# Shared SBUF stretches filled ahead across three phases, smaller weight pieces for three chunks, and the sample tokens taken first

## What is computed

```python
xn = rmsnorm(x, p['g_mix'][l])
proj = xn @ p['w_in'][l]
mq, mk, mv, mo, mi, mf, aq, ak, av, gt = split_proj(proj)
li = mi + b_igate;  lf = log_sigmoid(mf + b_fgate)
h_m, C, n, m = mlstm(mq, mk, mv, li, lf, st_C, st_n, st_m, m_chunk)
h_m = rms(h_m) * g_mhead * sigmoid(mo)
q, k = rope(aq, pos), rope(ak, pos)
h_a, nk, nv = swa_attend(q, k, av, st_k, st_v, buf_valid, a_sinks, a_block)
ga, gb = split(sigmoid(gt))
x = x + (ga * (h_m @ w_a) + gb * (h_a @ w_b)) @ w_out
y, cbuf = conv_ffn(rmsnorm(x, g_ffn), st_conv, w_up, w_conv, b_conv, w_down)
x = rmsnorm(x + y, g_final)
```

## Time and profile before

| | us |
|---|---|
| median of 3 runs | 3063.32 (3062.82 to 3065.42) |
| the profiled execution | 3068.29 |
| its span, first to last instruction | 3066.3 |
| PE busy | 2922.9 (95%) |
| PE weight loads busy | 2770.4 (90%) |
| VectorE busy | 1783.8 (58%) |
| ACT busy | 1390.4 (45%) |
| POOL busy | 649.2 (21%) |
| mean granted TensorE clock | 0.977 |

### The profile page before, as it was taken

One profiled execution on the slowest core, in us unless ns is written; L12 is line 12 of the kernel. 1 busy time (PEld: TensorE's weight loads), 2 busy tenths in 40 slices (PEclk: granted clock), 3 DMA queues, 4 the chain that ended last, 5 costly groups with the idle time before them and its releaser, 6 DMA issues.

```text
span 3066.3 us, 43381 instructions
## 1 busy us (share of the span) xinstructions
PE 2922.9 (95%) x16129; PEld 2770.4 (90%) x16129; DVE 1783.8 (58%) x2653; ACT 1390.4 (45%) x2432; POOL 649.2 (21%) x940
## 2 busy tenths in 40 slices
PE   5999969899999968999999999999999999999997
PEld 4888858888888968899999999999999999999996
DVE  3222146667766634765558755687646775477654
ACT  2222134545544423554446543465435555355443
POOL 1111011011111112211224211242112422124222
PEclk9999979999999989999999999999999999999998
DMA  4333265445454436344343453444443444333433
GB/s 139 116 104 104 71 195 187 146 147 169 146 168 137 144 114 201 101 163 128 117 144 125 153 165 121 138 139 147 156 142 128 141 144 146 122 117 119 138 116 78
DMA packets 242803, 419.67 MB, mean 137 GB/s; under 512 B 38563, under 2 KB 155683, under 8 KB 242595
## 3 DMA queue, kind: packets, MB, share of 16 engines
q1 hardware_dynamic: 240482, 416.77, 42.7%
q10 hardware_dynamic: 2112, 0.13, 0.0%
HBM read 352.12 MB, written 65.74 MB: 136 GB/s over the span
## 4 chain that ended last, share of the span: by engine, by line
PE 59%; DVE 1%; SPq 1%; issue 1%; DMA 1%; ACT 1%; POOL 0%; POOLq 0%; DVEq 0%; ACTq 0%
PE f_ps L1596 39%; PE f_ps L1601 19%; DMA f_sgi<-gate_rows 0%; PE f_st L1608 0%; SPq L1552 0%; SPq L1556 0%; SPq L1528 0%; DVE f_rinv L1808 0%; DMA f_raw<-in_w_out 0%; DVE f_ml L1803 0%; DVE f_xres L1812 0%; SPq L1510 0%; POOL f_sgi L1952 0%; DVE f_wl L1787 0%; ACT f_mh L1682 0%
## 5 line engine op out<-in xcount | busy, mean ns | idle before, releaser
L1787 DVE TENSOR_TENSOR f_wl<-f_raw,f_wh 128x1024 fp32r<-128x1024 f32 (+2 forms) x460 | 540.4, 1175 | 160.8 <-ACT f_wh L1652 154.9
L1596 PE MATMUL f_ps<-f_xh,f_wh 128*128 128x416 f32 x1760 | 617.9, 351 | 4.4 <-DVE f_xl L1821 4.3
L1596 PE MATMUL f_ps<-f_xl,f_wh 128*128 128x416 f32 x1760 | 618.6, 352 | 0.0
L1652 ACT ACTIVATE f_wh<-f_raw 128x1024 fp32r<-128x1024 f32 (+2 forms) x460 | 442.4, 964 | 292.5 <-PE f_ps L1601 274.6
L1601 PE MATMUL f_ps<-f_xh,f_wl 128*128 128x416 f32 x1760 | 367.6, 350 | 0.0
L1596 PEld LDWEIGHTS f_ps<-f_xh,f_wh 128*128 128x128 f32 x1760 | 330.0, 188 | 11.1 <-DVE f_xl L1821 6.7
L599 PE MATMUL pp<-gxh,gwh 128*128 128x416 f32 x800 | 303.5, 379 | 35.9 <-DVE gxl L576 35.9
L1596 PEld LDWEIGHTS f_ps<-f_xl,f_wh 128*128 128x128 f32 x1760 | 330.8, 188 | 3.9 <-issue 0.6
L1601 PEld LDWEIGHTS f_ps<-f_xh,f_wl 128*128 128x128 f32 x1760 | 329.9, 188 | 2.3
L1840 DVE SCALAR_TENSOR_TENSOR f_c<-f_u,f_taps,f_c 128x416 f32<-128x416 f32 (+2 forms) x264 | 154.3, 598 | 297.3 <-ACT f_c L1704 297.1
L1596 PE MATMUL f_ps<-f_gh,f_wh 128*128 128x416 f32 x880 | 310.9, 353 | 5.9 <-issue 5.9
(11 more groups left out here) (239 smaller groups left out, 5032.8 us busy)
## 6 DMA issues: line engine op xcount, KB each, us to landing
f_raw<-in_w_up SPq DMA_DIRECT2D x220, 512.0 KB, 3.6
f_raw<-in_w_dn SPq DMA_DIRECT2D x120, 384.0 KB, 3.0
graw<-in_w_gate SPq DMA_DIRECT2D x80, 512.0 KB, 4.0
gate_rows<-gsgo SPq DMA_DIRECT2D x100, 208.0 KB, 2.7
f_raw<-in_w_br SPq DMA_DIRECT2D x40, 512.0 KB, 3.8
f_raw<-in_w_out SPq DMA_DIRECT2D x40, 512.0 KB, 3.5
f_sgi<-gate_rows SPq DMA_DIRECT2D x80, 208.0 KB, 3.8
proj_rows<-a_out SPq DMA_DIRECT2D x17, 900.0 KB, 3.6
```

The lines of the kernel that those rows point to most:

```text
L1596: pe.matmul(ps[n][:, 0:TB], wh[s][:, (col + k) * P:(col + k) * P + P], x[:, k0 + k, :], start=(k == 0 and x is xhi), stop=False)
L1652: act.activation(wh[v % WS][:, 0:w], raw[s][:, 0:w], ACT.Copy).then_inc(ev("w_hi"), 1)
L1787: dve.tensor_tensor(wl[n][:, 0:w], raw[s][:, 0:w], wh[n][:, 0:w].bitcast(F32), ALU.subtract).then_inc(ev("w_lo"), 1)
```

## The change

**Memory.** Two stretches of SBUF (`low`, 6656 words per partition, and `high`, 9424) and the small `ghd` are allocated outside the phases. In A, `low` holds three weight buffers and `high` the chunk arrays; in B, `low` is the span and the three unit weights, and `high` the sample's arrays; in C, `low` is the residual and `high` weights, gated rows, heads, convolution buffers and one pair of gates. The semaphores of the next phase can be signalled from the one before (`next_ev`).

**Filling ahead.** In A, after chunk 8's normalised rows, SP loads B's first span and three unit weights into `low` (`ahead`). In B, after slot 4 of chunk 9, SP loads for C the output gates of the first span, `ghd`, the heads, three weights and a pair of gates; at the end of chunk 12 ACT takes the sigmoid and VectorE multiplies (`gated_act`, `gated_dve`). C's list then begins with the splits.

**Phase A.** Weights are taken in seven pieces of 256 columns (the last 264) through three buffers; each piece serves three chunks. The first chunk goes ahead with two pieces, the second column sum has a new place on VectorE, and the third chunk's column sum stands on PE behind the first product.

**Phase B.** The sample chunk is number 1 and the prompt chunks are 2 to 17; the 18 half units of the sample chunk now come first. Its arrays have their own place.

**Phase C.** The parameter loads and the residual move from SP's head into steps 5 and 2 of its loop.

The core of the diff:

```diff
-GROUP_A = 2
+GROUP_A = 3
+AHEAD_A = 8
+PIECES = [(c, s0 + c - c0, 264 if c == 1536 else 256) for c0, s0, w in ROWS for c in range(c0, c0 + w - 8, 256)]
+WRAWS = 3
...
-    raw = [sb(f"a_raw{i}", [P, KT, 512]) for i in range(2)]
+    raw = [k8(low[:, 2112 * i:2112 * i + 2112]) for i in range(WRAWS)]
...
+    G = GROUP_A
+    first = [(0, 0), (0, 1)] + [(n, j) for n in range(1, G) for j in range(2)] + [(n, j) for j in range(2, NP) for n in range(G)]
+    order = [(n, PIECES[j][0], PIECES[j][2], j + 1) for n, j in first] + [(n, c, w, NP) for n in range(G, N) for c, _, w in ROWS]
+    place = {u[0:2]: i for i, u in enumerate(order)}
...
+    end = len(first)
+    sum_at = {0: 2, end - 6: G, **{place[n - 1, ROWS[0][0]]: n for n in later}}
+    rows_at = {1: 2, end - 5: G, **{place[n - 1, ROWS[1][0]]: n for n in later}}
+    high_at = {end - 3: G, **{place[n - 1, ROWS[2][0]]: n for n in later}}
...
+        def ahead():
+            sp.wait_ge(ev("w_lo"), NP)
+            for q in range(2):
+                sp.wait_ge(ev(f"xn_out{q}"), 32)
+            sp.dma_start(low[:, 0:KT * TB].rearrange("p (k t) -> p k t", k=KT), xns[:, :, 0:TB]).then_inc(next_ev("gx_in"), 16)
+            for u in range(GRAWS):
+                at = KT * TB + KT * P * u
+                sp.dma_start(k8(low[:, at:at + KT * P]), a["w_mix"][:, :, C_MO + P * u:C_MO + P * u + P]
+                             ).then_inc(next_ev(f"gw_in{u}"), 16)
+        chunk_in(1)
+        weights(0)
+        weights(1)
+        chunk_in(2)
+        normed_out(0)
+        weights(2)
+        chunk_in(3)
+        normed_out(1)
+        for j in range(3, NP):
+            weights(j)
+            if j == 4:
+                normed_out(2)
+        for n in range(3, N):
+            chunk_in(n + 1)
+            normed_out(n)
+            if n == AHEAD_A:
+                ahead()
+            if n == 3:
+                for i in range(3):
+                    rows_out(i)
+            else:
+                rows_out(n - 1)
+        rows_out(N - 1)
...
+        reduce(0)
+        variance(0)
+        reduce(1)
+        normed(0)
+        variance(1)
+        x_low(0)
+        w_low(0)
+        normed(1)
+        x_low(1)
+        w_low(1)
+        reduce(2)
+        variance(2)
+        w_low(2)
+        normed(2)
+        x_low(2)
+        reduce(3)
...
-    for n in range(1, CHUNKS + 1):
+    for n in range(1, CHUNKS + 2):
         out[n] = []
-        for w in SLOTS:
+        for w in SLOTS if n > 1 else (3,) * LATE:
             out[n].append([half(h) for h in range(x, x + w)])
             x += w
-    w = (2 * GUNITS - x) // LATE
-    out[CHUNKS + 1] = [[half(h) for h in range(x + w * k, x + w * k + w)] for k in range(LATE)]
+    assert x == 2 * GUNITS
...
+AHEAD_B, GATED_B = 9, 12
...
+    N, S = CHUNKS + 1, 1
+    row_of = lambda n: n - 2 if n > S else CHUNKS
...
-        span_load(0)
-        for u in range(GRAWS):
-            unit_load(u)
...
+        sp.dma_start(kc, a["cache_k"]).then_inc(ev("kc_in"), 16)
+        sp.wait_ge(ev("m_ready"), 1)
+        sp.dma_start(m0[0:SAMP, :], a["state_m"]).then_inc(ev("m0_in"), 16)
         units(0, 0)
+        for h in range(MH):
+            r = DK * (h % 2)
+            sp.dma_start(cs[r:r + DK, h // 2], a["state_cn"][h]).then_inc(ev("cs_in"), 16)
+        sp.dma_start(vc.rearrange("p b g d -> p b (g d)"), a["cache_v"]).then_inc(ev("vc_in"), 16)
+        rows_load(S + 1)
...
+        def ahead():
+            for name, count in (("scn_out", 16 * MH), ("cs_ready", SEQS), ("cup_s", SEQS), ("pv_done", 2), ("sc_done", 2),
+                                ("inter_done", 1), ("kc_tr", 1), ("qbd_ready", 1), ("aqz_ready", 1)):
+                sp.wait_ge(ev(name), count)
+            sp.wait_ge(ev("hh_out0"), 48)
+            sp.wait_ge(ev("hh_out1"), 32)
+            for q in range(2):
+                sp.wait_ge(ev(f"sg_out{q}"), 48)
+            raws, gated, heads, gates, ghd = ahead_of_ffn(scratch)
+            sp.dma_start(gated, sgs[0, 0:MO].rearrange("f p t -> p f t")).then_inc(next_ev("sgm_in"), 16)
+            sp.dma_start(ghd, a["g_mhead"].rearrange("(k p) -> p k", p=P), allow_slow_non_contiguous=True).then_inc(next_ev("ghd_in"), 16)
+            for j in range(2):
+                sp.dma_start(heads[:, MO * j:MO * j + MO], hhs[:, MO * j:MO * j + MO, 0:TB]).then_inc(next_ev(f"hh_in{j}"), 16)
+            for v in range(RAWS):
+                sp.dma_start(raws[v].rearrange("p (s c) -> p s c", s=2), a["w_br"][v].rearrange("s p c -> p s c")
+                             ).then_inc(next_ev(f"w_in{v}"), 16)
+            for j in range(2):
+                sp.dma_start(gates[j], sgs[0, MO + j]).then_inc(next_ev("sg_in0"), 16)
...
+                if n == AHEAD_B and k == 4:
+                    ahead()
...
+    def gated_act(act):
+        act.wait_ge(next_ev("sgm_in"), 16)
+        gated = ahead_of_ffn(scratch)[1]
+        act.activation(gated, gated, ACT.Sigmoid).then_inc(next_ev("sgm_ready"), 1)
+    def gated_dve(dve):
+        _, gated, heads, _, ghd = ahead_of_ffn(scratch)
+        dve.wait_ge(next_ev("hh_in0"), 16)
+        dve.wait_ge(next_ev("ghd_in"), 16)
+        dve.wait_ge(next_ev("sgm_ready"), 1)
+        for k in range(MO):
+            dve.scalar_tensor_tensor(gated[:, k], heads[:, k], ghd[:, k:k + 1], gated[:, k], ALU.mult, ALU.mult
+                                     ).then_inc(next_ev("h_gated"), 1)
...
+        mix_pe_s(pe, S, 0)
+        mix_pe_a(pe, S, 0)
+        samp_pe_kc(pe)
+        units_pe(pe, S, 0)
+        mix_pe_last(pe, S, 0, "last_s")
+        samp_pe_scores(pe)
+        units_pe(pe, S, 1)
+        mix_pe_str(pe, S, 0)
+        samp_pe_inter(pe)
...
+def ahead_of_ffn(scratch):
+    high, at = scratch["high"], RAWS * KT * P
+    tile = lambda x, k: high[:, x:x + k * TB].rearrange("p (k t) -> p k t", k=k)
+    return ([high[:, KT * P * i:KT * P * i + KT * P] for i in range(RAWS)], tile(at, MO), tile(at + MO * TB, KT),
+            [high[:, AHEAD_G + TB * j:AHEAD_G + TB * j + TB] for j in range(2)], scratch["ghd"][:])
...
-        outgates_in(0)
-        sp.dma_start(ghd[:], a["g_mhead"].rearrange("(k p) -> p k", p=P), allow_slow_non_contiguous=True).then_inc(ev("ghd_in"), 16)
-        load(0)
-        half_in(0, 0)
-        half_in(0, 1)
-        gates_in(0, 0)
-        load(1)
         gates_in(0, 1)
-        load(2)
-        sp.dma_start(taps[:], a["taps"].rearrange("f p c -> p f c")).then_inc(ev("f_par"), 16)
-        sp.dma_start(gffn[:], a["g_ffn"]).then_inc(ev("f_par"), 16)
-        sp.dma_start(gfin[:], a["g_final"]).then_inc(ev("f_par"), 16)
-        residual(0)
-        for h in range(BLOCKS):
-            sp.dma_start(cst[:, h], a["conv_state"][h].rearrange("f p c -> p f c")).then_inc(ev("f_par"), 16)
         for v, (kind, b, i) in enumerate(PLAN):
             load(v + RAWS)
+            if v == 2:
+                residual(0)
+            if v == 5:
+                sp.dma_start(taps[:], a["taps"].rearrange("f p c -> p f c")).then_inc(ev("f_par"), 16)
+                sp.dma_start(gffn[:], a["g_ffn"]).then_inc(ev("f_par"), 16)
+                sp.dma_start(gfin[:], a["g_final"]).then_inc(ev("f_par"), 16)
+                for h in range(BLOCKS):
+                    sp.dma_start(cst[:, h], a["conv_state"][h].rearrange("f p c -> p f c")).then_inc(ev("f_par"), 16)
...
-        act.wait_ge(ev("fones_ready"), 1)
-        outgates(0)
-        high(0)
-        for k in range(KT):
+        h_high(0, 0)
+        w_high(0)
+        for k in range(1, KT):
             h_high(0, k)
-        high(1)
+        w_high(1)
...
+        h_low(0, 0)
+        w_low(0)
+        for k in range(1, KT):
+            h_low(0, k)
...
+    with ExitStack() as outer:
+        for name, width in (("low", 2 * KT * TB), ("high", HIGH), ("ghd", MO)):
+            scratch[name] = outer.enter_context(nc.sbuf_tensor("both_" + name, [P, width], F32))
+        phase(project_phase, ev_a, ev_m)
+        nc.clear_and_free_semaphores(list(all_a.values()))
+        nc.all_engine_barrier()
+        phase(mixer_phase, ev_m, ev_f)
+        nc.clear_and_free_semaphores(list(all_m.values()))
+        nc.all_engine_barrier()
+        phase(ffn_phase, ev_f, None)
```

573 lines of the change are left out of this document (284 added, 289 removed).

## The result

Beside four runs of the kernel before, with a median of 3064.37 us (3062.82 to 3067.09), the changed kernel took 3029.54 us (3028.95 to 3031.12, four runs). The ratio is 0.9884, with a 95% interval of 0.987 to 0.9898: 35 us, 1.2%, faster. The forecast was 3027, with a range of 3010 to 3045. The profiled execution of the changed kernel has a span of 3027.9 us and took 3029.81.

The account below looks back on a forecast made before the run. PE is busy 95% of the span, so only its stands can yield: the ramp and the heads of B and C. Terms summed to -36.2 on 3066.3; 2.0 around the span and 5.0 down to the median gave 3027 us, range 3010 to 3045.

Parts of the forecast that it names:

- Phase A: Ramp at the start: first product 9.8 us earlier, stand of 7.65 gone, new stand of 4.4; sum -13.0 (-17 to -9).
- A to B: Crossing into B: ACT need not wait for the span of x; -7.4 us of the 20.10 idle.
- Inside B: Sample chunk at the head, switches between spans, gate work and second filling: together +2 us (-2 to +12).
- the 1 us of a cold sample chunk: Head of B: cost of a cold pipeline with the sample chunk first, 1 us (0 to 6).
- 1 us of chunk 12: In B: cost of the added sigmoid, table loads and four products in that chunk, 1 us (0 to 5).
- B to C: Crossing into C: shorter tail -5.3, PE sooner after C's begin -9.5; sum -14.8 us (-17 to -11).
- The front of C: From PE's start in C to its second output product, with parameter loads moved: -3 us (-11 to +3).
- d: Front of C: time the parameter loads take on SP ahead of gates 7; taken as 10 to 12 us, 16 before.
- (c): Rival: the filling does nothing, B and C still start on something else; -19, 3044 us; chance 0.06.
- (d): Rival, slower: half clock stays through the sample chunk in B, up to 78 us more, in full 3105; chance 0.04.
- (b): Rival: queues take back part, front of C +3 and inside B +12; -20, 3043 us; chance 0.18.
- (a): Rival, more won: norm_sum(2) doesn't hold PE, parameters issue quickly; A -17.4, front of C -11; about 3011; chance 0.13.

Follow-up runs that it names:

- e7: Kernel before with only VectorE's order in the ramp of A changed to the changed kernel's: 3058.75 us (one run).
- e3: Changed kernel without its filling ahead, B's and C's loads and the gate work being back at each phase's own start: 3046.68 us.
- e5: Changed kernel with the output gates' sigmoid and four multiplies moved from chunk 12 of B back to C's head: 3033.58 us.
- e1: Changed kernel with the five parameter loads of C issued at step 9 of SP's loop in place of step 5: 3024.20 us.
- e2: Changed kernel with the reduce of chunk 2 ahead of the low half of weight piece 1 on VectorE: 3028.19 us (one run).
- e8: e1 with the weight load of step 9 also issued in step 5, ahead of the gates of product 7: 3022.15 us (one run).
- e1b: Changed kernel with step 5's gates load issued ahead of the five parameter loads, which stay in step 5: 3027.00 us (one run).
- e11: Changed kernel with only the taps' load moved from step 5 to step 9 of SP's loop: 3024.57 us (one run).
- e4: Changed kernel with dummy products on PE, results unread, ahead of the first product of each phase: 3027.24 us.
- e10: Changed kernel with e2, e8, B's first splits piece by piece, three dummy products at B's head, and two adds on VectorE instead of POOL: 3017.97 us.

## Why the prediction was right, step by step

**Phase A**, forecast -13.0, measured -13.6. First product 16.8 forecast, 16.58 measured; the new stand for norm_sum(2) 4.4, measured 4.55, for the reason given (the reduce queued behind the low half of piece 1); the old stand of 7.65 gone. "The loads of the pieces are taken at nothing" was right for this order of loads, and e7 shows what it costs if the chunk stands behind the weights: VectorE stood 5.3 us. Half clock "twice before, twice after" came to nothing, as put.

**A to B**, forecast -7.4, measured -7.2 (20.10 to 12.94). e3 gives the cause: without the filling it is 20.21.

**Inside B**, forecast +2, measured -2.0 from B's first product to its end (724.25 to 722.23). Kernels with the same B vary by 2 around their middle, so this says only that the +2 can't be seen. For the 1 us of a cold sample chunk, PE's list of waits shows nothing new behind B's first product: 3.6 us for the gates and 4.6 for the rotated queries, both there before too (the 4.6 in the earlier trace rows). For the 1 us of chunk 12, e5 shows that it was nothing (units within 0.2 us). That the stretch came out 4 us below the forecast for it has no cause that I can name. The upper bound of +12 was far too careful. The switches between spans did exchange stands as put, 15.8 us in four before and 27.5 less 12.9, 14.6, after.

**B to C**, forecast -14.8, measured -15.4, and both halves as worked out: the phase's begin 10.25 to 4.7 us after PE's end (-5.5; forecast -5.3), and PE 14.2 to 4.3 after that (-9.9; forecast -9.5). e3 and e5 name the causes of the second: the loads ahead are 6.5 and the gate work ahead is 4.1. The first, the tail, is put down to the sample chunk's place from SP's rows.

**The front of C**, forecast -3, measured 0 (57.46 before and 57.5 after; to the column sum 93.41 and 93.32). This is the step that was mis-sized. The mechanism was right: the gates of unit 7 stand behind the parameters, and f_ml grew to 11.4 where I had named about 10. Its terms were not. The request for gates 6 came at 29.9 after PE's start, not 27, with 1.3 for its issue and a weight's, not 0.5; d was 7.5, not 10 to 12; the gates took 4.6 to land and be taken up, not 3; and from there to the second output product were 14.1 us, not 12.6. Together 57.4, where 27.5 + 11 + 3 + 12.6 gave 54.1: d was 3.5 too large, and the other terms 2.9, 0.8, 1.6 and 1.5 too small. The reason for taking d below 16 was sound: with less queued ahead of them the taps landed 5.8 us after their issue instead of 9.8, and the load held behind them took 4.40 instead of 7.84. What PE won on the way (it reached the first output product 5.3 us earlier, 38.2 after its start against 43.5) it lost again on f_ml (+5.0). e1 shows that this was to be had: 4.7 us by the column sum, 5.5 from the first output product.

**The sum**: -36.2 forecast on the span, -38.4 measured; A -0.6, A to B +0.2, inside B -4, B to C -0.6, the front +3 against the forecast. Two misses, in B and in C, cancel in part, and that is luck: with C's front as measured and B as forecast, the time would have come 4 us higher, at 3033.5. A third lies outside the kernel: I took over the 5.0 us by which the profiled execution of before stood above its median. The changed kernel's stood 0.3 above (3029.81 against 3029.54), so its median came 2.5 above the forecast although its span came 2.2 below.

**The rivals.** (c), the filling does nothing, falls by e3. (d) falls by the windows, though the clock was not at 1.00 throughout, as the prediction's last part had it, but fell once more at 454 to 463, as it had before in the same products. (b) was half right in C: -3 became 0, not +3, and B gave nothing back. (a) is what e2 and e1 make of the changed kernel: its two conditions, the sum not in PE's way and the parameters out of the way, were worth 2.2 and 4.7 us when they were made true, not 6.4 and 8.

## What to carry to other kernels

Between two phases of one kernel the time goes to loads that could have been issued earlier, and memory shared by both phases is what allows it; each part of the crossing (last store, first load, work on the loaded data, order of the first splits) has its own price and is read from who released the first instruction. When small loads are moved off a head, look at what stands behind them on the queue in the new place: here five parameter loads, harmless data, took 5 us back because a load with a due time was queued behind them (e1). And count such a stretch from the last point at which two kernels still agree: C's first products alone differ by 0.7 us between kernels with the same code. Where a stand goes, a second limit of nearly its length often stands behind it, as in e1, e8 and e2: cost the next one before writing down the gain.

## What the runs showed of the hardware

A load made of very many small pieces holds the issuing of the next one on its queue. Behind the taps (88 KB in runs of 32 bytes) a 4 KB load took 7.84 us to issue in the kernel before, 4.40 in the changed kernel, 7.42 in e1, 8.08 in e8 and 2.33 in e1b, and 0.43 without the taps ahead of it (e11). In e11, where a 512 KB weight load was next behind the taps, that one took 5.93. The hold is no constant: in all six it ended 0.9 to 1.0 us before the taps had landed, which was 9.8, 5.8, 8.9, 9.7, 3.8 and 9.1 us after their issue. So it grows with what the taps themselves have to wait for.

PE's clock kept its upper level over a short stand after work: in e4, 2.44 us idle after the dummies, at 1.00 before and after. In the sample chunk it fell to its lower level behind small products (32 by 64, 129 columns) and a stand of only 0.35 us: 0.50 over 454 to 463 in the changed kernel and over 1103 to 1113 before, with PE busy throughout. And taking the half clock off a phase's head was worth something only where PE is what is late: in B (2.8 us by the sixth unit in e4), not in A and not in C.

The addition of two tiles of 416 columns took 1.08 to 1.94 us on POOL and 0.59 on VectorE (e10).
